# Hybrid decoder trunk: splitting the projection weights on GpSimd instead of ScalarE and VectorE, with two buffers, and an earlier sum of squares

## The reference, cut to what matters

```python
h = rmsnorm(x, norm1_g)
proj = h @ w_in                    # z | x,B,C | dt | q | k | v | q_mem
u_z, u_xbc, u_dt, q_sb, k_sb, v_sb, q_mem = split(proj)
y_ssd = ssd_mixer(u_z, u_xbc, u_dt, ...)             # causal conv, SiLU, scan
y_sb  = rmsnorm(stick_breaking_attention(q_sb, k_sb, v_sb))   # 6 heads
y_mem = rmsnorm(memory_cross_attention(q_mem, mk, mv))        # 4 heads
x = x + concat(y_ssd, y_sb, y_mem) @ w_out
h2 = rmsnorm(x)
x = x + peer_ffn(h2, ...)          # product-key retrieval over 16384 experts
```

## Time and profile before

| | us |
|---|---|
| median of 3 runs | 1527.31 |
| lowest, highest | 1526.39, 1529.0 |
| profiled execution, its own time | 1529.0 |
| its span (first to last instruction) | 1527.3 |
| PE busy | 1488.3 (97%) |
| DVE busy | 1184.9 (78%) |
| ACT busy | 699.3 (46%) |
| POOL busy | 308.3 (20%) |

### The profile page before, as it was taken

The page is one execution under the profiler, slowest core; times in us unless marked ns, Lnnn a source line. Parts: engine busy times, 40 slices in busy tenths (PEclk is TensorE's granted clock), DMA queues, the critical chain, the costliest instruction groups (busy, mean ns, idle before and its releaser), DMA issues.

```text
span 1527.3 us, 23442 instructions
## 1 busy us (share of the span) xinstructions
PE 1488.3 (97%) x7883; PEld 1303.5 (85%) x7883; DVE 1184.9 (78%) x2156; ACT 699.3 (46%) x1235; POOL 308.3 (20%) x296
## 2 busy tenths in 40 slices
PE   7999989988999999999999999999999999999998
PEld 4877755668999999999999999988888888888887
DVE  7454463588998899888998884687878878788885
ACT  5453652123357854578346773433333333333331
POOL 1000100006013211222112242242222222132210
PEclk9999999989999999999999999999999999999999
DMA  7120304027778897689867999899999999999993
GB/s 289 43 70 0 139 0 166 1 111 260 232 240 293 322 357 230 224 317 351 314 224 245 346 363 387 328 386 349 355 323 339 354 321 362 331 377 359 344 353 148
DMA packets 170146, 403.00 MB, mean 264 GB/s; under 512 B 14049, under 2 KB 95969, under 8 KB 168033
## 3 DMA queue, kind: packets, MB, share of 16 engines
q1 hardware_dynamic: 133216, 268.01, 49.0%
q0 software_dynamic: 36864, 134.23, 25.0%
HBM read 347.67 MB, written 54.53 MB: 263 GB/s over the span
## 4 chain that ended last, share of the span: by engine, by line
PE 89%; DVE 5%; DMA 3%; ACT 1%; issue 1%; POOL 1%; SPq 0%; DVEq 0%; ACTq 0%
PE psum L507 55%; PE psum L1037 34%; DMA uraw<-in_uT 2%; DMA urow<-in_u,eidx 1%; POOL urow L485 1%; DMA wring<-in_chunks 0%; DVE urow L1761 0%; DVE ulo L1755 0%; DVE memT L1596 0%; ACT pr L1220 0%; DVE x L1633 0%; DVE sco L1820 0%; PE psum L769 0%; DVE hlo L1743 0%; DVE mstat L1668 0%
## 5 line engine op out<-in xcount | busy, mean ns | idle before, releaser
L507 PE MATMUL psum<-hhi,uhi 128*128 128x384 f32 x1024 | 347.7, 340 | 1.7 <-ACT act_s L1374 1.7
L507 PE MATMUL psum<-hlo,uhi 128*128 128x384 f32 x1024 | 343.0, 335 | 0.0
L1450 ACT ACTIVATE vhi<-vraw 128x1024 fp32r<-128x1024 f32 x128 | 135.9, 1062 | 330.8 <-PE psum L1037 330.8
L485 POOL DMA_INDIRECT urow<-in_u,eidx x128 | 154.9, 1210 | 594.1 <-DVE urow L1761 413.2
L1037 PE MATMUL psum<-vhi,whi 128*128 128x512 f32 x768 | 236.6, 389 | 0.0
L1037 PE MATMUL psum<-vhi,wlo 128*128 128x512 f32 x768 | 236.4, 389 | 0.0
L1037 PE MATMUL psum<-vlo,whi 128*128 128x512 f32 x768 | 236.4, 389 | 0.0
L1957 DVE TENSOR_TENSOR vlo<-vraw,vhi 128x1024 fp32r<-128x1024 f32 x128 | 156.6, 1223 | 77.1 <-ACT vhi L1450 77.1
L485 POOL DMA_INDIRECT urow<-in_v,eidx x120 | 132.3, 1102 | 372.6 <-DVE acc L1963 366.8
L507 PE MATMUL psum<-hhi,ulo 128*128 128x384 f32 x1024 | 199.4, 336 | 3.9 <-DVE ulo L1755 3.9
L507 PEld LDWEIGHTS psum<-hhi,uhi 128*128 128x128 f32 x1024 | 193.1, 189 | 2.8 <-ACT uhi L1367 2.3
(11 more groups left out here) (294 smaller groups left out, 1837.9 us busy)
## 6 DMA issues: line engine op xcount, KB each, us to landing
uraw<-in_uT SPq DMA_DIRECT2D x128, 512.0 KB, 5.6
vraw<-in_v SPq DMA_DIRECT2D x128, 512.0 KB, 6.1
acts_scratch<-act_s SPq DMA_DIRECT2D x128, 192.0 KB, 3.8
gates_scratch<-stage SPq DMA_DIRECT2D x12, 2048.0 KB, 9.9
gring<-gates_scratch SPq DMA_DIRECT2D x32, 768.0 KB, 8.8
aring<-acts_scratch SPq DMA_DIRECT2D x128, 192.0 KB, 6.1
wring<-in_chunks SPq DMA_DIRECT2D x20, 512.0 KB, 5.4
wout<-in_wout SPq DMA_DIRECT2D x1, 4096.0 KB, 12.7
```

What stands on the lines that cost most here:

```text
L485: g.indirect_dma_start(urow[k], None, table, bass.IndirectOffsetOnAxis(eidx[:, n % HK:n % HK + 1], 0)).then_inc(row_in[k], 16)
L507: return nc.tensor.matmul(out, lhsT, rhs, start=start, stop=stop)
L1450: a_(vhi[:, k, :], vraw[:, k, :], ACT.Copy).then_inc(s["vhi_ready"], 1)
```

## The change

POOL makes both halves. For each split chunk i it waits for the chunk's load, and from i = 2 on for the end of the job that used chunk i-2; it adds zero to the weights into `bhi` (rounded), waits for that itself, and subtracts into a separate tile `blo`. Both have two buffers instead of four and the ring slot. `upper_chunks` on ACT and `lower_chunks` on DVE, with all their calls, are gone. PE reads `blo` instead of `wringlo`. And PE computes the sum of squares `ssqx` behind xbc1 instead of xbc2, and rowx behind xbc2 instead of xbc3.

```diff
-JOBS = (["xbc0", "xbc1", "xbc2", "ssqx", "xbc3", "rowx", "xbc4"] + ...
+JOBS = (["xbc0", "xbc1", "ssqx", "xbc2", "rowx", "xbc3", "xbc4"] + ...
...
-bhi = [at(kib, f"bhi{k}", [P, DC, P], F32R)[:] for k, kib in enumerate((5, 9, 111, 115))]
-wringlo = at(63, "wringlo", [P, RING, DC, P], F32R)
+bhi = at(5, "bhi", [P, 2, DC, P], F32R)
+blo = at(111, "blo", [P, 2, DC, P], F32R)
...
 # gpsimd, behind the constants
+zero = iota16[:, 0:1].broadcast_to([P, DC * P])
+for i, n in enumerate(SPLIT):
+    pool.wait_ge(w_in[n % RING], 16 * (n // RING + 1))
+    if i >= 2:
+        full(pool, LAST_USE[SPLIT[i - 2]])
+    w = wring[:, n % RING].rearrange("p c n -> p (c n)")
+    hi, lo = bhi[:, i % 2].rearrange("p c n -> p (c n)"), blo[:, i % 2].rearrange("p c n -> p (c n)")
+    g.tensor_tensor(hi, w, zero, ALU.add).then_inc(s["bhi_ready"], 1)
+    pool.wait_ge(s["bhi_ready"], i + 1)
+    g.tensor_tensor(lo, w, hi.bitcast(F32), ALU.subtract).then_inc(s["blo_ready"], 1)
 full(pool, LAST_USE[SPLIT[-1]])
...
 # tensor
 for c in range(DC):
-    mm(o, bhi[i % 4][:, c, :], xhi[:, c, :], c == 0, False)
-    mm(o, bhi[i % 4][:, c, :], xlo[:, c, :], False, False)
+    mm(o, bhi[:, i % 2, c, :], xhi[:, c, :], c == 0, False)
+    mm(o, bhi[:, i % 2, c, :], xlo[:, c, :], False, False)
 pe.wait_ge(s["blo_ready"], i + 1)
 for c in range(DC):
-    last = mm(o, wringlo[:, n % RING, c, :], xhi[:, c, :], False, c == DC - 1)
+    last = mm(o, blo[:, i % 2, c, :], xhi[:, c, :], False, c == DC - 1)
...
 for i in range(CC):
     x_channels("xbc", i)
+    if i == 1:
+        squares_x()
     if i == 2:
-        squares_x()
-    if i == 3:
         to_rows("rowx", "ssqx", rsB, NT)
...
 # scalar: the function and its eight calls go
-def upper_chunks(*which):
-    for i in which:
-        n = SPLIT[i]
-        act.wait_ge(w_in[n % RING], 16 * (n // RING + 1))
-        if i >= 4:
-            full(act, LAST_USE[SPLIT[i - 4]])
-        a_(bhi[i % 4], wring[:, n % RING], ACT.Copy).then_inc(s["bhi_ready"], 1)
...
 # vector: the function and its calls go
-def lower_chunks(*which):
-    for i in which:
-        dve.wait_ge(s["bhi_ready"], i + 1)
-        v.tensor_tensor(wringlo[:, SPLIT[i] % RING], wring[:, SPLIT[i] % RING], bhi[i % 4].bitcast(F32),
-                        ALU.subtract).then_inc(s["blo_ready"], 1)
```

More of the change, by code:

```diff
@@ L147 @@
         ("K", 3), "ssqm", "mk0", ("V", 1), ("Z", 2), "mk1", "rowm", "mv0", "mv1", ("K", 4), "mkss0", "mkss1", "qmss", ("K", 5)]
-JOBS = (["xbc0", "xbc1", "xbc2", "ssqx", "xbc3", "rowx", "xbc4"] + [f"v{t}" for t in range(NT)] + ["q0", "k0"]
+JOBS = (["xbc0", "xbc1", "ssqx", "xbc2", "rowx", "xbc3", "xbc4"] + [f"v{t}" for t in range(NT)] + ["q0", "k0"]
         + [name for item in PROJ for name in (sb_jobs(*item) if isinstance(item, tuple) else [item])]
@@ L192, in trunk @@
         memg, mqg, mkg = par[:, 50:52], par[:, 52:53], par[:, 53:54]
-        bhi, h2row = [at(kib, f"bhi{k}", [P, DC, P], F32R)[:] for k, kib in enumerate((5, 9, 111, 115))], at(5, "h2row", [P, 2, D])
+        bhi, h2row = at(5, "bhi", [P, 2, DC, P], F32R), at(5, "h2row", [P, 2, D])
         xhi, x1 = at(13, "xhi", [P, DC, T], F32R), at(13, "x1", [P, NT, D])
@@ L200, in trunk @@
         wring, wout = at(63, "wring", [P, RING, DC, P]), at(63, "wout", [P, DC, D])
-        wringlo = at(63, "wringlo", [P, RING, DC, P], F32R)
-        xlo, memT = at(95, "xlo", [P, DC, T], F32R), at(119, "memT", [P, DC, M])
+        xlo, blo, memT = at(95, "xlo", [P, DC, T], F32R), at(111, "blo", [P, 2, DC, P], F32R), at(119, "memT", [P, DC, M])
         rmB, zT, cin = at(127, "rmB", [P, M]), at(128, "zT", [P, SC, T]), at(134, "cin", [P, CC, T + CONV - 1])
@@ L1073, in _ @@
                 a_(sq[:, c % 2, :], xT[:, c, :], ACT.Square).then_inc(s["sq_ready"], 1)
-            upper_chunks(0, 1)
             act.wait_ge(s["wv_in"], 16)
@@ L1077, in _ @@
             a_(vwhi[:], wv[:], ACT.Copy).then_inc(s["vwhi_ready"], 1)
-            upper_chunks(2, 3)
             act.wait_ge(s["consts"], 1)
@@ L1093, in x_tokens @@
                 free(a_(dts[:, 0, t, :], o[:, SB_W:VD], ACT.Copy, scale=rowr[:, t:t + 1]), f"v{t}")
-            upper_chunks(4, 5, 6)
             for t in range(NT):
@@ L1139, in weights @@
                 a_(zs[:, h % 2, :], zs[:, h % 2, :], ACT.Exp).then_inc(s["sb_w"], 1)
-            upper_chunks(7, 8)
             front(0)
             upper_nk(0)
-            upper_chunks(9, 10)
             upper_nk(1)
             weights(0)
-            upper_chunks(11, 12)
             weights(1)
@@ L1152, in _ @@
                 a_(sqm[c], memT[:, c, :], ACT.Square).then_inc(s["memsq_ready"], 1)
-            upper_chunks(13)
             front(1)
@@ L1497, in _ @@
                     v.tensor_tensor(rsB[:], rsB[:], a, ALU.add).then_inc(s["sq_used"], 1)
-            lower_chunks(0, 1)
             dve.wait_ge(s["vwhi_ready"], 1)
             v.tensor_tensor(vwlo[:], wv[:], vwhi[:].bitcast(F32), ALU.subtract).then_inc(s["vwlo_ready"], 1)
-            lower_chunks(2)
             dve.wait_ge(s["consts"], 1)
@@ L1515, in _ @@
                 ins.then_inc(s["conv_ready"], 1)
-                lower_chunks(*((3,), (4,), (5,), (6,), ())[i])
             dve.wait_ge(s["wdt_in"], 32)
@@ L1564, in _ @@
             scaled("q", 1, qT)
-            lower_chunks(7, 8)
             scaled("k", 1, kT)
@@ L1570, in _ @@
             scaled("q", 2, qT)
-            lower_chunks(9, 10)
             argument(0)
@@ L1575, in _ @@
             argument(1)
-            lower_chunks(11, 12)
             scaled("z", 0, zT)
@@ L1583, in _ @@
                 v.tensor_tensor(rmB[:], sqm[0] if c == 1 else rmB[:], sqm[c], ALU.add).then_inc(s["memsq_added"], 1)
-            lower_chunks(13)
             scaled("z", 1, zT)
```

## The result

| | before | after |
|---|---|---|
| median, us | 1528.15 (1526.39 to 1529.41, 4 runs) | 1544.85 (1541.46 to 1548.82, 4 runs) |
| ratio | | 1.010 (95%: 1.0085 to 1.0116) |
| profiled execution: span, us | 1527.3 | 1544.0 |

The changed kernel is 1.0% slower: 16.7 us by the medians, and 16.7 us between the spans of the two profiled executions. The ratio with its interval says 15.3 us (13.0 to 17.7). The forecast was 13.7 us more (1541 us), with a range from 1530 to 1547 us.

The account below looks back on a forecast made before the run. The prediction took PE, busy for 97% of the span, to bound the kernel. It added 8.2 us at the start and 5.5 us at the first pair of heads, 13.7 us, to the 1527.3 us median: 1541 us, range 1530 to 1547 us.

Parts of the forecast that it names:

- kT: DVE's kT of the first pair of heads: costed at nothing, up to 2 us if it collides with POOL too.
- the third head: Lower nk of the third head: 3.1 us of slack against delays of at most 2.7 us, so no cost.
- What leaves ACT and DVE: Halves removed from ACT (14.3 us) and DVE (16.7 us) are off PE's path: gain 0, at most 3.5 us.
- POOL's price: Each of POOL's 28 operations of 128x1024 takes 1.96 us, 3.9 us a chunk; buffers and rate cost nothing.
- A collision: Each POOL operation of 1024 columns that meets DVE's work delays DVE by 1.7 us (1.4 to 1.96 us).
- Place 1: The start: four collisions delay the adds into rsB; PE waits 6.7 us plus 1.5 us of clock, 8.2 us.
- Place 2: First pair of heads: POOL delays not_kept and lower nk; PE waits 4.0 us plus 1.5 us of clock, 5.5 us.
- Instructions with an input in PSUM: kT, the argument and the scaling by rsB read PSUM and one SBUF input: costed at nothing.
- B: Rival: only the start stalls, DVE getting its turn first at the first pair of heads; 1535.5 us, chance 0.20.
- C: Rival: POOL too slow for PE, at 3.5 us an operation 15 to 20 us more, 1558 us; chance 0.08.
- D: Rival: no collision that matters, rsB ready at 23.3 us and PE unbroken; 1527 us, chance 0.11.
- E: Rival: relief of ACT and DVE ends memT's scaling earlier, gaining up to 3.5 us; 1524 us, chance 0.04.

Follow-up runs that it names:

- e6_dummy_read: Kernel before with the early sum of squares, halves left on ACT and DVE, plus 24 useless POOL additions of 128x1024 that read SBUF: ratio 1.0091.
- e9_all_waits: Changed kernel, sum of squares in its old place, POOL's k2 halves held behind the first lower nk and its scan products behind memT's scaling: ratio 1.0012.
- e10_pool_last: Changed kernel, POOL's first upper half held behind DVE's last square, k2's halves behind the first lower nk, scan products behind memT's scaling: ratio 1.0000.
- e11_sega_again: Second run of the kernel before with POOL's scan products held until DVE has scaled memT: ratio 0.9983, 2.6 us faster.
- e8_sega_late: Kernel before with POOL's scan products held until DVE has scaled memT: ratio 0.9986, 2.1 us faster.
- e4_wait_nk: Changed kernel with POOL starting the halves of chunk k2 only when DVE has made the first lower nk: ratio 1.0056.
- e3_early_ssq: Kernel before with only the sum of squares and rowx moved forward, halves still on ACT and DVE: ratio 0.9998.
- e1_old_ssq: Changed kernel with the sum of squares and rowx back in their old places, POOL still making both halves: ratio 1.0056.

## Why the prediction was right, point by point

- **The number.** The mechanism and both places are as forecast. The size is at the edge: the worked bounds end at 15.7 us, and the medians differ by 16.7 us. The 4 us by which the range goes beyond them were meant for kT and for the third head, and neither cost anything, so the room that the 16.7 us needed came from terms that stayed at zero. That part is luck. The ratio (15.3 us, 13.0 to 17.7) fits the forecast of 13.7 us.
- **What leaves ACT and DVE: gain 0.** Right. In e6_dummy_read the 31 us were still on ACT and DVE and the loss was the same size; and with the collisions mended, e9_all_waits and e10_pool_last are no faster than the kernel before.
- **POOL's price, 1.96 us each.** Right for the upper half (1.89 us), too low for the lower half (2.39 us). The sum of both was 4.3 us instead of 3.9. Their mean is 2.14 us. Buffers and rate cost nothing: right, PE has no wait for a half.
- **A collision costs DVE 1.7 us.** Right in sum: the adds took 12.39 - 5.47 = 6.9 us more against 4 x 1.7 = 6.8 us. Two errors offset each other: the operations were longer than 1.96 us (8.6 us for the four), and DVE lost 0.8 of their length instead of 0.87. The price had been read from memT with the undisturbed scaling taken as 2.7 us for eight; e11_sega_again shows 2.2 us, so 2.2 us and not 1.7 us were lost there, 0.9 of POOL's 2.4 us. The way there was different, too: I had the first collisions on xlo, but xlo kept its 4.90 us and POOL's first operation waited 3 us for the end of it. All four fell on the adds.
- **Place 1, 8.2 us (wait 6.7 us, clock 1.5 us).** 8.9 us. The adds ended at 30.6 us, forecast 30.1 us. PE waited 5.8 us and not 6.7 us, since it arrived 1.4 us later than before, behind slower first weight loads. That is no effect of the change: the last such load starts at 13.25 us in e8_sega_late, which up to there is the kernel before, and at 10.4 us in e4_wait_nk, with POOL's halves. Nor does the late arrival add to the loss, because the adds end when they end: in e4_wait_nk PE arrived at 23.4 us, waited 6.9 us, and reached kT of the first pair at 79.6 us, as late as the changed kernel (79.4 us). Behind the wait the half clock cost about 1.7 us. e3_early_ssq shows that the early sum of squares is free by itself, and e1_old_ssq that it adds to the cost under collisions.
- **Place 2, 5.5 us (wait 4.0 us, clock 1.5 us).** 6.5 us: wait 4.7 us, clock about 1.8 us. The pattern is the one forecast, three operations of POOL against three of DVE in turn. The wait was mis-sized by 0.7 us: the forecast took 4.0 us between a block of three operations (5.0 us) and of two (2.3 us), and POOL's third operation got in fully. e4_wait_nk shows that nothing else is behind it.
- **Instructions with an input in PSUM cost nothing.** Right: cin at 53.89 us.
- **The third head's slack holds.** Right: no wait of PE there.
- **Rivals.** B (start only) fell by the 4.7 us wait, C (POOL too slow) by the missing waits for halves, D (no collision) by the adds. E's mechanism, relief of DVE, gave nothing; but the 3.5 us which I put as its limit are real and belong to another cause, POOL's products over memT, of which e8_sega_late and e11_sega_again got 2.1 and 2.6 us.

Two things stay open: why DVE's eight xlo operations kept POOL out to the last one while adds and not_kept took turns with it, and whether e9_all_waits loses its gain at the start in some executions.

## What to carry to other kernels

Before work goes to GpSimd, look at what VectorE does at that time: here each GpSimd operation that read SBUF took 0.8 to 0.9 of its length from VectorE instructions with two SBUF inputs or from TENSOR_SCALAR with one, and that costs time where VectorE's result has no slack. So list the places where TensorE takes a VectorE result within a microsecond, and keep GpSimd out of them by a semaphore wait on GpSimd, if it has the time to give. Here it gave 5 us at the first pair of heads and 3 us at memT for nothing, but at the start a delay of some 9 us made TensorE wait 2.6 us for the first halves. Moving a consumer forward to where its input is "just ready" is free only as long as the producer isn't delayed: 5.8 us of slack behind the sum of squares were given up for nothing, and then needed (and even they would have left a wait of 2.6 us, as e1_old_ssq shows).

## What the runs showed that I had not expected

- The lower half (two full SBUF inputs) takes 2.39 us on GpSimd and the addition of a broadcast zero 1.89 us, a copy 1.04 us, a fill 0.96 us, all of 128x1024.
- A fill by GpSimd, which only writes, left VectorE's two-input instructions exactly as they were (5.47 us for seven adds), but a one-input TENSOR_SCALAR beside a fill took 0.93 us instead of 0.55 us.
- The block holds GpSimd up as much as VectorE: 4.96 us instead of 1.89 us under xlo, 5.54 us instead of 2.39 us under vwlo.
